# High and low weight slots moved behind the activations at the top of the partition

## The reference

```python
h = _rmsnorm(x, g_mix); proj = h @ w_in                 # 12 + 4 + 4 + 4 + 4 + 16 weight tiles
...
x = x + mixed @ w_out
x = x + (jax.nn.silu(h @ w1) * (h @ w3)) @ w2
x = x + gate * (p_i @ w_ple)
...
u = jnp.take(expert_u, expert, axis=0)                  # peer_ffn, once in each layer
act = jax.nn.gelu(jnp.einsum('thkd,td->thk', u, xc))
w = (g * act).astype(xc.dtype)
return jnp.einsum('thk,thkd->td', w, jnp.take(expert_v, expert, axis=0))
```

## Time and profile before

| what | value |
|---|---|
| time, median of 3 runs | 2530.08 us (2529.55 to 2531.4) |
| the profiled execution | 2528.41 us, of which the span from first to last instruction is 2526.6 us |
| mean granted PE clock | 0.983 of full speed |
| busy | PE 2449.4 us (97%), PEld 2270.9, DVE 1831.6, ACT 1243.6, POOL 1230.3 |

### The profile page before, as it was taken

How to read it: one execution, slowest core, us unless ns; L and a number is a source line. 1 busy time by engine, 2 the same in 40 slices (tenths; PEclk the granted TensorE clock), 3 DMA queues, 4 the chain that set the end, 5 groups by cost and what they waited for, 6 DMA issues and landing times.

```text
span 2526.6 us, 47107 instructions
## 1 busy us (share of the span) xinstructions
PE 2449.4 (97%) x18074; PEld 2270.9 (90%) x18074; DVE 1831.6 (72%) x3372; ACT 1243.6 (49%) x2142; POOL 1230.3 (49%) x525
## 2 busy tenths in 40 slices
PE   7999999989899999999999999999999999999999
PEld 7998999988899999997888888889999999888887
DVE  6758683668749899987767765563997999555555
ACT  6335543456555544444444455555454444444444
POOL 5547687654679977760000014456997777100000
PEclk9999999989899999999999998999999999999999
DMA  5326697732456654547877763335665545566664
GB/s 169 134 89 191 197 334 257 281 118 82 136 176 192 199 157 154 159 151 261 256 258 252 260 195 109 101 109 150 194 192 176 157 154 156 183 191 192 192 192 142
DMA packets 126064, 457.94 MB, mean 181 GB/s; under 512 B 13985, under 2 KB 15393, under 8 KB 125601
## 3 DMA queue, kind: packets, MB, share of 16 engines
q1 hardware_dynamic: 118512, 425.56, 53.8%
q10 hardware_dynamic: 7344, 29.49, 3.4%
HBM read 453.95 MB, written 1.05 MB: 180 GB/s over the span
## 4 chain that ended last, share of the span: by engine, by line
PE 86%; DVE 8%; issue 2%; ACT 2%; POOL 1%; DMA 1%; SPq 0%; DVEq 0%; POOLq 0%; ACTq 0%
PE mm L1294 28%; PE ms L1334 28%; PE mm L812 18%; PE ms L1315 3%; POOL low L1930 1%; DVE work L1987 1%; DVE hs L1987 1%; PE ms L819 1%; PE ms L827 1%; DVE scratch L1987 1%; PE mm L980 1%; DVE mm L1981 1%; PE mm L819 1%; PE mm L859 0%; PE ms L1076 0%
## 5 line engine op out<-in xcount | busy, mean ns | idle before, releaser
L1930 POOL TENSOR_TENSOR low<-ring,high 128x1024 fp32r<-128x1024 f32 (+2 forms) x502 | 1216.5, 2437 | 917.5 <-ACT high L1545 759.6
L1795 ACT ACTIVATE high<-ring 128x1024 fp32r<-128x1024 f32 x506 | 535.8, 1059 | 355.7 <-PE ms L1334 319.9
L1294 PE MATMUL mm<-hs,high 128*128 128x256 f32 x4096 | 520.3, 280 | 3.4 <-ACT high L1545 3.4
L1334 PE MATMUL ms<-high,wts 128*128 128x512 f32 x2048 | 510.5, 391 | 0.0
L2557 DVE TENSOR_TENSOR low<-ring,high 128x1024 fp32r<-128x1024 f32 x256 | 313.3, 1225 | 248.3 <-ACT high L1795 248.2
L1294 PEld LDWEIGHTS mm<-hs,high 128*128 128x128 f32 x4096 | 486.7, 188 | 3.8 <-issue 3.8
L1334 PEld LDWEIGHTS ms<-high,wts 128*128 128x128 f32 x2048 | 384.2, 188 | 83.9
L1545 ACT ACTIVATE high<-ring 128x1024 fp32r<-128x1024 f32 (+2 forms) x252 | 258.2, 1030 | 135.8 <-PE mm L812 111.7
L812 PE MATMUL mm<-hs,high 128*128 128x256 f32 x2224 | 290.1, 284 | 4.1 <-ACT high L1545 2.8
L812 PEld LDWEIGHTS mm<-hs,high 128*128 128x128 f32 x2224 | 271.8, 192 | 9.0 <-ACT high L1545 4.9
L1334 PE MATMUL ms<-low,wts 128*128 128x512 f32 x1024 | 276.5, 392 | 3.0 <-DVE low L2557 3.0
(11 more groups left out here) (341 smaller groups left out, 3062.9 us busy)
## 6 DMA issues: line engine op xcount, KB each, us to landing
ring<-w_peer_experts SPq DMA_DIRECT2D x512, 512.0 KB, 4.2
work<-w_mod ACTq DMA_DIRECT2D x48, 512.0 KB, 4.9
ring<-w_late_mods SPq DMA_DIRECT2D x48, 512.0 KB, 4.6
ring<-w_ffn_up SPq DMA_DIRECT2D x44, 512.0 KB, 4.7
ring<-w_peer_q SPq DMA_DIRECT2D x32, 512.0 KB, 3.7
ring<-w_fox_in SPq DMA_DIRECT2D x32, 512.0 KB, 3.5
ring<-w_lru_in SPq DMA_DIRECT2D x22, 512.0 KB, 3.5
ring<-w_gates SPq DMA_DIRECT2D x16, 512.0 KB, 3.5
```

Source lines behind the costliest of these rows:

```text
L1294: ins_ = pe.matmul(mm[:, s_ % BANKS, 0:T], w_[:, k * P:(k + 1) * P], hs[:, b_, k, :], start=pass_ == 0 and k == 0, stop=pass_ == 2 and k = ...
L1334: ins_ = pe.matmul(ms[:, 2 * c + half, :], wts[:, s_ % 3, b_, c * P:(c + 1) * P], v_[:, half * 512:(half + 1) * 512], start=s_ == 0 and pa ...
L1795: act.activation(high[:, (q0 + i) % CUT, :], ring[:, n_ % RAW, :], ACT.Copy) \
L1930: pool.tensor_tensor(low[0:rows, cut_slot, 0:width], ring[0:rows, raw_slot, 0:width], high[0:rows, cut_slot, 0:width].bitcast(F32), ALU.su ...
```

## The change

`high` and `low`, 12288 bytes each, are allocated last in place of second. Shapes, slots and everything that reads or writes them stay.

```diff
         ring = sb("ring", [P, RAW, SLOT])
 
-        high = sb("high", [P, CUT, SLOT], F32R)
-        low = sb("low", [P, CUT, SLOT], F32R)
         x = sb("x", [P, KD, T])
...
         wts = sb("wts", [P, 3, 2, T], F32R)
+        high = sb("high", [P, CUT, SLOT], F32R)
+        low = sb("low", [P, CUT, SLOT], F32R)
```

## The result

The changed kernel takes 2580.15 us (median of 4, 2578.04 to 2582.5) against 2529.82 us beside it, a ratio of 1.0198 (95% interval 1.0185 to 1.021): 50.3 us slower. The forecast was 2530 us, so it missed.

The account below looks back on a forecast made before the run. PE's cadence times its matmuls was taken as the bound (busy 2449.4 of 2526.6 us). All terms summed to 0 on the profiled 2528.41 us, giving 2530 us for the median, range 2522 to 2541 us.

Parts of the forecast that it names:

- Step 1: PE's weight loads from `high` and `low` in L812 and L1294: near operands cost nothing, taken as 0.
- rival B: L812, perhaps L1294's long pieces: PE's two reads now meet, slow cadence becomes the rule; 2544 to 2554 us, 17%.
- Step 5: PE's restart after interruptions, L812 and L1294: cadences dealt anew, 9.2 us less to 13.7 plus 10.1 us more, taken as 0.
- the 39.5 us: The slower case's extreme end, all of L1294 slow too (25.8 us in place of 10.1), which the prediction did not believe.
- Step 2: Values stage L1334, moved slots streaming against `wts`: taken as 0, with at best 5.8 us less (229.1 to 227.2 ns).
- Steps 3 and 4: ACT's writes to `high` and subtractions into `low` keep their times; DMA lands as before or in time: 0 each.
- rival D: L1294: POOL's subtraction, with 0.33 us to spare per tile, becomes the bound; 26 us more, 2556 us, 3%.
- Rival C: L812 wholly fast (9.2 us) and values at 227.2 ns (5.8 us): faster, 2515 us, half expected at 2522 us; 15%.

Follow-up runs that it names:

- e2: The changed kernel with 64 unused bytes ahead of `high`, so hs - high is 192 modulo 256 again: ratio 0.9998 to before.
- e13: The changed kernel with 64 unused bytes ahead of `wts`, giving hs - high 192 and wts - high 0: 2523.28 us, 0.9974 of before.
- e3: The kernel before with 64 unused bytes ahead of `work`, moving `work`, `hs` and `wts` but not `high`, both distances 0: ratio 1.0197 to before.
- e5: The kernel before with 32 unused bytes ahead of `high` and 96 behind `low`, both distances 32: 2572.98 us, ratio 1.015 to before.
- e7: The kernel before with 64 unused bytes between `high` and `low` and 64 behind `low`, only `low` at distance 0: 2565.61 us, ratio 1.0117 to before.
- e15: The kernel before with slots of `high` and `low` 16 bytes further on and a [P, 56] pad ahead of `high`, all distances 208: ratio 1.0217 to before.
- e4: The kernel before with 64 unused bytes ahead of `wts` alone, hs - high 192 and wts - high 0: 2520.66 us, 0.9961 of before.
- e8: e4 with 128 more unused bytes behind `low`, giving hs - high 64 and wts - high 128: ratio 1.0137 to before.
- e11: The kernel before with a pad of 224 bytes behind `low`, both distances 160: ratio 1.0193 to before.
- e1: The kernel before with 64 unused bytes ahead of `high` and 64 behind `low`, both distances 0, operands far apart: ratio 1.0192 to before.
- e12: The kernel before with 160 unused bytes behind `low` and 160 ahead of `wts`, hs - high 96 and wts - high 0: ratio 1.0195 to before.

## Why the prediction was wrong

**Step 1 failed, and with it the sum.** It priced PE's weight loads from the moved slots at 0, by showing that operands that lie near each other are not slower. That is true (e2, e13), but it answers another question: what counts is the distance modulo 256 bytes. It went from 192 to 0, and that costs 6.6 ns in each matmul at the fast cadence. The rows used as evidence were float32 and bf16 matmuls, and step 1 itself left float32r open. They could not have shown it: the float32 ones of L1272 do not react when the distance from `ring` to `work` goes from 192 to 0 (e3, the last section), and the bf16 ones have both operands in one tensor, whose distance no run changes.

**An argument against rival B was unsound.** It said that loaded blocks step by 512 bytes and streamed ones by 1024, so that the relative position changes all the time without a trace. Both steps are multiples of 256. `hs`, `work` and `wts` all stood at 192 against `high` and `low`, and so the trace was all but silent on the very number that the change moved. One exception went unread: the matmuls with 258 columns step through `raw` by 1032 bytes, so their remainder varies from one to the next. They also hardly reacted, which would fit a mixture of remainders (argued, not tested): `raw,low` with 258 columns went from 286 to 287 ns, while `raw,high` with 256 columns went from 279 to 285 ns, and L812's largest group with 258 columns has the same row in both profiles:

```profile
L812 PE MATMUL mm<-raw,high 128*128 128x258 f32 x192 | 25.1, 283 | 0.2 <-ACT work L1872 0.2
```

**Step 5 had the right suspect and bounds that were too narrow.** It named the two remainders and asked whether being in step plays a part, and it took the price from the two cadences that the trace showed, at most 117.9 ns. The chip has more than two: 120.2 ns stands in no row of before. The bound was 13.7 + 10.1 = 23.8 us where L1294 alone cost 37.6 us. The price of a cadence that the trace did not contain could not be bounded by the two that it did, and the 39.5 us that I called unbelievable was less than what came. The share of slow pieces was misread too: from recorded lengths it took at most 2 in 5 of L812's matmuls as slow, but of the five pieces of 66 in the chain of before four are at 7.77 us and one at 7.49.

**Step 2** had the sign and size of its lower bound about right: 229.1 to 226.9 ns, 6.8 us against the 5.8 us given, though it was taken as 0. The bound came from doubling the fast cadence and not from any view of the distance, so its nearness is luck.

**Steps 3 and 4 held.** PE's waits for the moved tensors did not grow, and ACT and DVE write in the same time; the rows of after that answer to the earlier trace rows:

```profile
L1795 ACT ACTIVATE high<-ring x506: 1050/1061/1065, 757.6 to 2564.4; 128x1024 fp32r<-128x1024 f32 x169
L1930 POOL TENSOR_TENSOR low<-ring,high x502: 1012/2430/4506, 10.4 to 2215.3; 128x1024 fp32r<-128x1024 f32 x166, 128x384 fp32r<-128x384 f32 x2
L2557 DVE TENSOR_TENSOR low<-ring,high x256: 1218/1226/1227, 1172.3 to 2565.5; 128x1024 fp32r<-128x1024 f32 x128
```

POOL is 33 ns slower, far from rival D's 0.33 us, and nothing waits for it. **Rival B** had the right stages and the right direction with the wrong cadence and price (117.7 ns, 2544 to 2554 us). **Rival C** had the values stage right and L812 wrong.

The Trainium skill, in "TensorE: Matmul & The Clock Gate" (Part 2) and "SBUF — State Buffer" (section "Who interferes with whom"), gives PE two independent read ports and lets it wait for nobody; neither of these sections speaks of addresses, and the zero for the placement that the prediction drew from them does not hold here: the same loads and the same matmuls differ by 6% in cadence when only addresses move. The measurement decides. That the two reads of PE meet in some part of the memory that repeats every 256 bytes would fit the table, but it is argued and not shown, and the two cadences at one distance (e5, e7, e15) ask for something more: no run separates the weight load's read from the streamed read.

What stays open: why the cadence goes up and down so unevenly over the distances; why one distance can have two cadences (in L1294 or L812 at 32, 64, 160 and 208, but in no kernel at 0); and what puts a piece of L812 into the 117.7 ns cadence at distance 192. That mix is still there in the fastest versions (in e4, one of five pieces of 66 is at 7.49 us, the others at 7.77).

## What to carry to other kernels

Where PE is the bound, divide a long unbroken piece of the chain by its count and compare with the same shape elsewhere, and then try pads of 32 to 64 bytes between the tensors that are loaded as weights and those that stream: here they move the time by 2.4% one way and 0.4% the other without touching an instruction. When a change moves addresses, work out the remainders of the distances between operands that are used together, by 256 and not only by the alignment of each; and when nearly all of the trace has one value of such a number, it says nothing on the others, whatever bounds its rows suggest. Measure each pad: of the distances tried for L1294 only 192 kept its long pieces at 113.6 ns, and 16 bytes to either side of it cost 4.4 to 5.4 ns in each matmul.

## What the runs showed of the hardware

Cadence of float32r matmuls with 128 loaded columns and 256 streamed ones, both in SBUF, by the distance from weights to activations (L1294, the first layer's long piece, ns): 0: 120.2, 32: 116.9, 64: 118.0, 96: 120.2, 128: 118.9, 160: 117.6, 176: 119.0, 192: 113.6, 208: 118.0, 224: 118.6. With 512 streamed columns, by the distance from the streamed weights to the loaded `wts` (L1334): 0: 226.9, 32: 233.5, 96: 234.5, 128: 233.5, 160: 233.5, 176: 231.3, 192: 229.1, 208: 233.5, 224: 233.5. Both distances are modulo 256 bytes. The best place of the one is not that of the other. In L1294 and in L812's pieces of 66, distance 0 had one cadence; at others the same distance gave two: 116.9 and 118.0 ns at 32 (the two layers of e5), 118.0 (e8) and 113.1 ns (the high passes of e7) at 64, and in L812 117.4 and 120.0 ns at 160 (e11, pieces of 66 at 7.75 and 7.92 us) and 113.5 and 117.7 ns at 192. Neither the place in the partition nor the distance in kilobytes changed a cadence: 113.6 ns at 182 KB (before) and at 22.6 KB (e2), 120.2 ns at 182 KB (e1) and at 22.5 KB (after). The values repeat to 0.03 us in 137 us between kernels of the same distances, at 192 and at 0.

The float32 matmuls of L1272, loaded and streamed from `ring` and `work`, did not react: 64 of them take 7.38 us in before and after (distance of the two tensors' starts 192 modulo 256), in e3 (0) and in e12 (96). The row of e3:

```profile
744.59 7.38 PE L1273 MATMUL mm<-ring,work 128*128 128x128 f32 x64 [0.68 <-ACT work L1555]
```

The bf16 matmuls of L1315 have both operands in `onehots`, so their distance is the same in every kernel: 12 of them take 0.66 us in after (910.44 to 911.10 us, below) and 0.65 us in before, which says nothing on how bf16 reacts to a distance.

```profile
910.44 0.84 PE L1315 MATMUL ms<-onehots 128*128 128x128 bf16 x12
911.10 1.08 PE L1294 MATMUL mm<-hs,high 128*128 128x256 f32 x7
```
